# Expert blocks of 64 tokens kept as two halves of 32 and turned on VectorE, with four column groups on TensorE

## The reference, cut to what matters

```python
def expert_block(args):                       # MOE_BLOCK rows of one expert
    xe, e = args
    return (jax.nn.silu(xe @ w_gate[e]) * (xe @ w_up[e])) @ w_down[e]

yb = lax.map(expert_block, (xb.reshape(n_blocks, MOE_BLOCK, dm), blk_expert)).reshape(-1, dm)
y_slot = yb[dest] * wts.reshape(-1)[order][:, None].astype(x.dtype)
return jax.ops.segment_sum(y_slot, tok, num_segments=n_tok)
...
x = x + gate2 * ffn.reshape(bsz, L, D_MODEL)
y_sample = rmsnorm(xs, norm_f_w)
```

## Time and profile before

| | us |
|---|---|
| median of 3 runs | 1439.46 (1433.66 to 1447.06) |
| the profiled execution | 1438.59 |
| its span in the trace | 1436.8 |
| router done, first block's gate products begin | 744.4 |
| last block's down products end | 1406.9 |
| TensorE busy | 1337.9 (93%) |
| VectorE, ScalarE, GpSimd busy | 414.1, 263.3, 235.1 |

### The profile page before, as it was taken

How to read it: one execution, slowest core, us unless ns; L and a number is a source line. 1 busy time by engine, 2 the same in 40 slices (tenths; PEclk the granted TensorE clock), 3 DMA queues, 4 the chain that set the end, 5 groups by cost and what they waited for, 6 DMA issues and landing times.

```text
span 1436.8 us, 25808 instructions
## 1 busy us (share of the span) xinstructions
PE 1337.9 (93%) x10155; PEld 837.8 (58%) x10156; DVE 414.1 (29%) x886; ACT 263.3 (18%) x401; POOL 235.1 (16%) x285
## 2 busy tenths in 40 slices
PE   5899999977999999999958999999999999999975
PEld 3688778756676677764434455555555555454532
DVE  4692870375622210113362000000000000000065
ACT  3305002243125000001111111111111111111102
POOL 0033403200000000000023022012022222223310
PEclk9899999998999999999979999999999999999997
DMA  7459632345430412514088619819949999999993
GB/s 303 150 130 391 149 71 68 80 148 194 148 131 3 177 44 78 215 39 167 15 336 343 257 44 383 340 29 350 393 151 398 379 403 381 404 379 397 383 401 122
DMA packets 92365, 322.30 MB, mean 224 GB/s; under 512 B 12000, under 2 KB 12384, under 8 KB 91536
## 3 DMA queue, kind: packets, MB, share of 16 engines
q1 hardware_dynamic: 72304, 268.77, 49.5%
q0 software_dynamic: 11216, 38.41, 8.7%
q10 hardware_dynamic: 8784, 14.24, 3.2%
HBM read 286.18 MB, written 33.10 MB: 222 GB/s over the span
## 4 chain that ended last, share of the span: by engine, by line
PE 72%; DMA 13%; DVE 5%; issue 3%; SPq 3%; ACT 2%; POOL 0%; POOLq 0%; DVEq 0%; ACTq 0%
PE ps L2236 18%; PE ps L1771 11%; PE ps L2247 10%; PE ps L1759 9%; DMA expert_w<-in_w_down 9%; PE ps L2150 5%; PE ps L2199 5%; SPq L557 3%; PE ps L1863 2%; PE ps L1946 2%; DMA expert_w<-in_w_up 2%; PE ps L2242 1%; DMA x_sorted<-h,router_ints 1%; PE ps L1832 1%; PE ps L2226 1%
## 5 line engine op out<-in xcount | busy, mean ns | idle before, releaser
L2236 PE MATMUL ps<-expert_w,x_block_t 128*64 128x256 f32 x3584 | 403.8, 382 | 15.1 <-issue 6.5
L2236 PEld LDWEIGHTS ps<-expert_w,x_block_t 128*64 128x64 f32 x3584 | 256.0, 137 | 163.1 <-issue 31.5
L2247 PE MATMUL ps<-expert_w,act_t 128*64 128x512 f32 x896 | 213.9, 604 | 3.6 <-DMA expert_w<-in_w_down 2.6
L1771 PE MATMUL ps<-h_t,weight_ring 128*128 128x320 f32 x640 | 178.4, 435 | 0.0
L1771 PEld LDWEIGHTS ps<-h_t,weight_ring 128*128 128x128 f32 x640 | 121.5, 191 | 50.9 <-issue 2.8
L1759 PE MATMUL ps<-h_t,weight_ring 128*128 128x320 f32 x512 | 145.4, 447 | 2.8 <-ACT h_t L749 2.8
L1669 DVE TENSOR_TENSOR activations<-silu_tmp,ps 128x256 f32<-128x256 f32 x56 | 23.6, 421 | 375.9 <-ACT silu_tmp L967 375.9
L1759 PEld LDWEIGHTS ps<-h_t,weight_ring 128*128 128x128 f32 x512 | 100.1, 197 | 45.2 <-issue 6.9
L2247 PEld LDWEIGHTS ps<-expert_w,act_t 128*64 128x64 f32 x896 | 57.8, 136 | 103.1 <-issue 78.2
L692 POOL COPY expert_w<-staged 128x1024 f32<-128x1024 f32 x42 | 43.9, 1044 | 414.5 <-PE ps L2236 269.0
L1690 DVE COPY y_block<-ps 128x512 f32<-128x512 f32 x25 | 17.3, 692 | 188.7 <-PE ps L2247 188.7
(11 more groups left out here) (362 smaller groups left out, 1224.2 us busy)
## 6 DMA issues: line engine op xcount, KB each, us to landing
expert_w<-in_w_down SPq DMA_DIRECT2D x128, 512.0 KB, 13.2
weight_ring<-in_stream SPq DMA_DIRECT2D x98, 512.0 KB, 4.9
expert_w<-in_w_gate SPq DMA_DIRECT2D x58, 512.0 KB, 11.8
expert_w<-in_w_up SPq DMA_DIRECT2D x58, 512.0 KB, 12.8
staged<-in_w_gate SPq DMA_DIRECT2D x28, 512.0 KB, 14.0
gathered<-in_w_gate SPq DMA_DIRECT2D x28, 512.0 KB, 16.0
gathered<-in_w_up SPq DMA_DIRECT2D x28, 512.0 KB, 16.5
x_sorted<-zero POOLq DMA_DIRECT2D x18, 512.0 KB, 13.8
```

What stands on the lines that cost most here:

```text
L1771: last = mm(pair(job)[:, a, :], w[:, k, :], h_t[:, k, a * HALF:(a + 1) * HALF], start=(k == 0), stop=(k == KD - 1))
L2236: last = mm(ps[MB * g:MB * g + MB, 2 * half + w, 0:256], x_blk_t[:, 2 * kp + k2, :], rows[:, at_col:at_col + 256], start=(kp == 0 and k2 = ...
L2247: last = mm(ps[MB * half:MB * half + MB, 4, :], act_t[:, 4 * (f // 4) + 2 * (f % 2) + f // 2 % 2, :], w_slot[3 * f + 2][:, 4 * half:4 * ha ...
```

## The change

A block stays 64 tokens, but as two halves h of 32 (`SUB`). The token operand is 32 columns wide and four column groups (`Q`) run side by side. `gates(h, k)` is four matmuls of 512 columns, which stream 256 columns of the up weight and 256 of the gate weight of input chunk k in one instruction (`w_pair`). Both halves use each chunk in turn, but for the last two, where half 0 uses both and then half 1 both. `down(h, j)` is four matmuls of 256 columns: half 0 with chunks 0 to 3, half 1 with chunks 0 to 3, then both halves in turn with each of chunks 4 to 7. Every output feature of a half now needs all eight input chunks.

The turns of tokens and activations move to VectorE's transpose of 32 x 32 squares: `turn_act(h)` behind each product and `turn_x()` behind both. The rows of the weights are permuted on the host (`expert_rows`) so that these squares put the features where they are needed; ScalarE's three copies per block go. The tokens are loaded, and the results stored, as 128 partitions of 1 KB per half where it was 64 partitions of 2 KB per column half. TensorE's last two blocks are written out like those of the other engines, with `down_both(j)` (two column groups of 64, 512 columns) behind both activations, and the ten selection matrices are turned in the first of the two. For the very first block, VectorE turns the picked tokens straight from PSUM.

```diff
-            def turn_x():
-                for j in range(4):
-                    last = nc.tensor.transpose(ps[:, 6, j * P:(j + 1) * P], x_blk[:, j * P:(j + 1) * P], ident)
-                last.then_inc(xt_done, 1)
-            def turn_act(a):
-                for j in range(2):
-                    last = nc.tensor.transpose(ps[:, 5 + 2 * a, j * P:(j + 1) * P], acts[:, a, j * P:(j + 1) * P], ident)
-                last.then_inc(act_turned, 1)
...
+            def gates(h, k):
+                for g in range(Q):
+                    last = mm(ps[SUB * g:SUB * g + SUB, h, :].rearrange("p (w c) -> p w c", w=2), x_blk_t[:, h, k, :],
+                              w_pair[k][:, :, QC * g:QC * g + QC], start=(k == 0), stop=(k == KD - 1))
+                if h == 1:
+                    last.then_inc(gu_done, 1)
+                elif k == KD - 1:
+                    last.then_inc(half_done, 1)
+
+            both = KD - 2
+            tail_gates = [(0, k) for k in range(both, KD)] + [(1, k) for k in range(both, KD)]
+            tail_downs = [(h, j) for j in range(KF // 2, KF) for h in range(2)]
+
+            def down(h, j):
+                for g in range(Q):
+                    last = mm(ps[SUB * g:SUB * g + SUB, 4 + h, 0:QC], act_t[:, j, h, :],
+                              w_down_sb[j][:, QC * g:QC * g + QC],
+                              start=(j == 0), stop=(j == KF - 1))
+                if h == 1:
+                    last.then_inc(down_done, 1)
+
+            def down_both(j):
                 for half in range(2):
+                    last = mm(ps[MB * half:MB * half + MB, 4, :], act_t[:, j, :, :].rearrange("p h t -> p (h t)"),
+                              w_down_sb[j][:, 512 * half:512 * half + 512],
+                              start=(j == 0), stop=(j == KF - 1))
                 last.then_inc(down_done, 1)
...
             with pe.Fori(1, NBLK) as i:
-                with pe.If(i < blocks):
+                with pe.If(i < last2):
...
+                    for k in range(both):
+                        wait_gates(e, k)
+                        gates(0, k)
+                        gates(1, k)
+                    for h, k in tail_gates:
+                        if h == 0:
+                            wait_gates(e, k)
+                        gates(h, k)
+                    pe.wait_ge(act_ready, i * 2 + 1)
+                    pe.wait_ge(y_copied, i + 1)
+                    for j in range(KF // 2):
+                        pe.wait_ge(dn_in[j], e * 16 + 16)
+                        down(0, j)
+                    pe.wait_ge(act_ready, i * 2 + 2)
+                    for j in range(KF // 2):
+                        down(1, j)
+                    for h, j in tail_downs:
+                        if h == 0:
+                            pe.wait_ge(dn_in[j], e * 16 + 16)
+                        down(h, j)
                 pe.nop()
...
+            for u in range(2):
...
+                pe.wait_ge(y_copied, last2 + (u + 1))
+                if u == 0:
+                    pe.wait_ge(pick_ready, 1)
+                    for n in range(2 * CH):
+                        last = nc.tensor.transpose(ps[:, (7, 5, 6)[n // 4], (n % 4) * P:(n % 4 + 1) * P],
+                                                   pick[:, n // CH, n % CH, :, :].rearrange("p a t -> p (a t)"), ident)
+                    last.then_inc(pick_turned, 1)
+                pe.wait_ge(act_ready, last2 * 2 + (2 * u + 2))
+                for j in range(KF):
+                    pe.wait_ge(dn_in[j], e * 16 + 16)
+                    down_both(j)
...
+            def turn_act(h):
+                vec.transpose(act_t[:, :, h, :], acts[:, h, :].rearrange("p (j l) -> p j l", l=SUB)).then_inc(act_ready, 1)
+
+            def turn_x():
+                vec.transpose(x_blk_t[:, :, :, :].rearrange("p h k t -> p (h k t)"),
+                              x_blk[:, :, :].rearrange("p h c -> p (h c)")).then_inc(xt_copied, 1)
...
             for u, (ahead, beside, behind) in enumerate(((0, 0, 6), (3, 6, 5))):
                 add_some(ahead)
-                dve.wait_ge(silu_ready, last2 * 2 + (2 * u + 1))
-                take_prod(0)
-                add_some(beside)
-                dve.wait_ge(silu_ready, last2 * 2 + (2 * u + 2))
-                take_prod(1)
+                for h in range(2):
+                    dve.wait_ge(silu_ready, last2 * 2 + (2 * u + h + 1))
+                    take_prod(h)
...
             def load_x(row):
-                for g in range(2):
-                    act.dma_start(x_blk[MB * g:MB * g + MB, :], x_sorted[bass.ds(row, MB), 512 * g:512 * g + 512])\
+                for h in range(2):
+                    act.dma_start(x_blk[:, h, :], x_sorted[bass.ds(row + SUB * h, SUB), :].rearrange("t (q c) -> q t c", q=Q))\
                         .then_inc(x_blk_in, 16)
```

More of the change, by code:

```diff
@@ L981, in _ @@
                 with act.If(i < last2):
[L982 to L988, removed]
+                    act.wait_ge(half_done, i + 1)
+                    take_gates(0)
+                    act.wait_ge(gu_done, i * KF + KF)
@@ L1006, in _ @@
[L1006 to L1009 removed]
+                act.wait_ge(half_done, last2 + (u + 1))
+                take_gates(0)
+                act.wait_ge(gu_done, last2 * KF + (u * KF + KF))
+                take_gates(1)
@@ L2223, in _ @@
             pe.wait_ge(pick0_ready, 1)
-            def turn_x():
-                for j in range(4):
-                    last = nc.tensor.transpose(ps[:, 6, j * P:(j + 1) * P], x_blk[:, j * P:(j + 1) * P], ident)
-                last.then_inc(xt_done, 1)
-            def gates(s):
-                half, kp = s // 4, s % 4
-                for k2 in range(2):
-                    for w in range(2):
-                        rows = w_slot[3 * s + w][:, :, :].rearrange("p k c -> p (k c)")
-                        for g in range(2):
-                            at_col = 512 * k2 + 256 * g
-                            last = mm(ps[MB * g:MB * g + MB, 2 * half + w, 0:256], x_blk_t[:, 2 * kp + k2, :],
-                                      rows[:, at_col:at_col + 256], start=(kp == 0 and k2 == 0), stop=(kp == 3 and k2 == 1))
-                last.then_inc(gu_done, 1)
@@ L2309, in _ @@
-                pe.nop()
-            pe.wait_ge(pick_ready, 1)
-            pe.wait_ge(xt_copied, blocks + 1)
-            pe.nop()
-            for n in range(2 * CH):
-                last = nc.tensor.transpose(ps[:, (7, 5, 6)[n // 4], (n % 4) * P:(n % 4 + 1) * P],
-                                           pick[:, n // CH, n % CH, :, :].rearrange("p a t -> p (a t)"), ident)
-            last.then_inc(pick_turned, 1)
+                    for k in range(both):
+                        wait_gates(e, k)
+                        gates(0, k)
+                        gates(1, k)
@@ new lines, in _ @@
+                    for h, j in tail_downs:
+                        if h == 0:
+                            pe.wait_ge(dn_in[j], e * 16 + 16)
+                        down(h, j)
+                pe.nop()
+            for u in range(2):
+                e = pe.value_load(rint[0:1, bass.ds(last2 + u, 1)], min_val=0, max_val=EXPERTS - 1)
+                pe.wait_ge(xt_copied, last2 + (u + 1))
+                for k in range(both):
+                    wait_gates(e, k)
+                    gates(0, k)
+                    gates(1, k)
+                for h, k in tail_gates:
+                    if h == 0:
+                        wait_gates(e, k)
+                    gates(h, k)
+                pe.wait_ge(y_copied, last2 + (u + 1))
+                if u == 0:
+                    pe.wait_ge(pick_ready, 1)
[7 more added lines that the diff above has]
+                    down_both(j)
```

222 lines of the change are left out of this document (96 added, 126 removed).

## The result

The changed kernel takes 1508.46 us (median of 4 runs, 1505.79 to 1516.67) against 1440.76 us for the kernel before on the same chip (median of 4): a ratio of 1.0481, 95% interval 1.0417 to 1.0545. It is slower by 4.8%; the prediction of 1432 us, with a range up to 1451, was wrong. The profiled execution took 1508.03 us with a span of 1506.0 us, 69.2 us more than the 1436.8 of before.

The account below looks back on a forecast made before the run. DMA was taken to bound most of the kernel, TensorE alone only 6.5 of 28 blocks. Terms of -0.3, -9.3, +2.5, +2.6, +1.5 and -4 summed to -7.0 us from 1438.59: 1431.6, said as 1432 for the median, range 1418 to 1451.

Parts of the forecast that it names:

- Tokens and results: Block loads and stores: 256 packets of 2 KB become 512 of 1 KB, 0.44 us more DMA time a block where DMA bounds.
- start: Up to 802.38, DMA bound: last chunk lands where it did, half a down chunk less behind it, -0.3 us.
- three cycles: DMA-bound cycles of two blocks and one: token packets add 1.3 us, a closing DMA gap saves 0.4, +0.9 us each.
- The period: TensorE's time per block: 20.9 us instead of 22.46, with four column groups overlapping; bounds 20.5 and 22.5.
- The turn is covered: Before down: silu, product and VectorE's turn take 1.62 us, just covered by 1.7 of matmuls; rival of no cover, 1442, chance 0.1.
- TensorE-bound stretches and transitions: Middle of the kernel: TensorE-bound stretches save 9.3 us together; three DMA-bound transitions lose 0.85 us each, +2.5.
- The packet's price: Token queue: a line through 4 KB and 2 KB packets gave 63 ns for 1 KB, 0.44 us more a block.
- The skipped iterations: Ahead of the last block but one: nine absent blocks skipped, 5.8 to 10 us of TensorE, 1 us lost.
- The last block: Second product only after six gathered operations, last product at 1412.1, first sum about 1416 against 1420.26: -4 us.
- cycles above 72 (packets): Sign of a wrong forecast: cycles of two blocks and one above 72 us, put down to packets.
- The sign at the end: Sign of a wrong forecast: first sum later after the last weights than the 27.5 us of before.

Follow-up runs that it names:

- e1_spread: Changed kernel with x_block loads and y_sorted stores cut by column group, on 16 DMA engines, same 1 KB packets: 1430.61 us, ratio 0.9931 to the kernel before.
- e5_before_1kb: Kernel before with each block's four transfers cut into eight of 64 x 1 KB, on 16 engines: 1440.4 us, ratio 1.0003.
- e9_before_eight: Kernel before with block loads and stores given an outer dimension of 8, packets still 2 KB: 1466.55 us.
- e7_bound: Changed kernel with transfers on 16 engines, and engine loops ended where the blocks end instead of skipping absent ones: 1429.53 us, ratio 0.9942 to the kernel before.
- e4_before_four: Kernel before with block loads and stores given an outer dimension of 4, packets still 2 KB: 1532.67 us.
- e6_tail: Changed kernel with transfers on 16 engines, and the last block's six gathered operations moved behind its second product: 1428.05 us, ratio 0.9907 to the kernel before.

## Why the prediction was wrong

The step that failed is the term "Tokens and results". It saw that 256 packets of 2 KB become 512 of 1 KB and divided their time by 16 engines ("6.9 us over 16 engines, 0.44 us more DMA time a block"). With 19 DMA-bound blocks that made some 8 us. The diff's `"t (q c) -> q t c"` changed the number of engines too, from 16 to 4, and no rival held that. Measured, this alone is worth 77.0 us, or 3.7 to 4.3 us a DMA-bound block (table below).

The term it should have had, from bytes and a rate of the runs: 4 transfers of 128 KB a block are 524 KB; on 16 engines each carries 33 KB, on four 131. At 386 GB/s over 16 engines (e1_spread's cycle; 391 in the earlier trace rows would do as well), 24.1 GB/s each, the 98 KB more are 4.1 us a block. The chains, stretch by stretch, from one listed block start to the next (second column: the changed kernel less e1_spread; third: the term times the DMA-bound blocks of the stretch; fourth: e1_spread less the kernel before; fifth: what the prediction had for that; all in us). The last row but one runs to the end of the spans, 1436.8 us before, 1506.0 changed and 1429.0 in e1_spread:

| stretch | 4 engines against 16 | by the term | e1_spread against before | predicted |
|---|---|---|---|---|
| start | +0.2 | | +2.0 | -0.3 |
| first transition, with the blocks before it | +9.1 | 2.5 x 4.1 = 10.3 | -2.0 | -2.75 |
| second | +10.7 | 10.3 | -2.5 | -2.75 |
| third | +10.1 | 10.3 | -1.35 | -1.2 |
| three cycles | +11.5, +11.4, +13.0 | 12.3 each | +1.2, +1.2, -0.05 | +0.9 each |
| last two blocks and end | +11.0 | | -6.35 | -2.5 |
| sum | +77.0 | | -7.8 | -6.8 |

The prediction's own sum says -7.0: it entered the three cycles as 2.6, where 3 x 0.9 is 2.7, and rounded twice more. The term needs nothing of the changed kernel but its diff. The 2.0 us at the start stand open, but the start is not firm: in the kernel before it is at 802.38, in e5_before_1kb at 802.37 and in e9_before_eight at 799.09. The starts on which the table rests, of the kernel before as far as the earlier trace rows doesn't have them, and of e1_spread:

```profile
1029.70 8.85 PE ps L2236 x80
...
1120.63 8.85 PE ps L2236 x80
...
1189.11 8.85 PE ps L2236 x80
...
1257.52 8.85 PE ps L2236 x80
```

```profile
804.38 13.94 PE ps L2233 x128
...
916.34 13.94 PE ps L2233 x128
...
1027.20 13.94 PE ps L2233 x128
...
1116.78 13.94 PE ps L2233 x128
...
1186.49 13.94 PE ps L2233 x128
...
1256.12 13.94 PE ps L2233 x128
...
1324.72 13.94 PE ps L2233 x128
```

The Trainium skill, "DMA: Bandwidth & Descriptors", section "Why a DMA increments its semaphore by 16 and not by 1", states the rule: the engines are the largest number up to 16 that divides the slowest dimension (of size above 1) of both access patterns. This case agrees, with 4, 8 and 16 closing packets for outer dimensions of 4, 8 and 32 or 64. The prediction weighed another section of the same page and passed over this one.

The other steps, with the transfers on 16 engines:

- The period: 20.9 forecast, 20.94 and 21.00 measured. Four column groups do overlap on records of 512 columns.
- The turn is covered: in a middle block TensorE is idle for 0.15 us of 21.00 (825.4 to 846.4). The transposes took 446 ns for 256 elements a partition, against the 0.42 assumed (L1659), and 672 ns for 512 (L1662). The prediction's estimate from the Trainium skill, VectorE: DVE Perf Modes, section "The three transpose paths", 0.62 us, was too high for this fp32 shape. Twice the elements took 1.5 times as long, so the time was not in proportion to them.
- TensorE-bound stretches and transitions: right within 0.8 us each in e1_spread. That its whole sum is near the forecast (-7.8 against -6.8) is in part luck: the end gave 3.9 us more than forecast, and the start took 2.3 us more.
- The packet's price: the sign was right and the size wrong, 0.03 us a block instead of 0.44 (e5_before_1kb). The straight line between a 4 KB weight packet and a 2 KB token packet made a fixed cost out of what is a difference between queues; within one queue (q10, 100 ns for 2 KB and 51 ns for 1 KB) the time went with the bytes. The Trainium skill, DMA: Bandwidth & Descriptors, section "Why small descriptors are slow (HBM only)", has the rule that the prediction set aside, by which two packets of 1 KB are an estimated 4% over one of 2 KB. This case agrees: 7.3% against 7.1%. e1_spread's cycles are still 1.2 us longer than before, twice of three, where e5's aren't (68.3, 68.6, 68.2); why was not settled.
- The skipped iterations: 6.41 us of idle time (5.8 to 10 forecast), 6.45 in e1_spread; their effect was put at 1 us, and the time of e7_bound can't tell it from nothing.
- The last block: the second product did wait for the six gathered operations. In e1_spread the first sum came at 1412.51, for the 1416 forecast. In the changed kernel it came only at 1489.43: the late gathers stood ahead of the product.
- In the tests for right and wrong: "cycles above 72 (packets)" named the right sign, and the wrong cause for it; e4_before_four and e5_before_1kb were needed to part them. The sign at the end came true as well: from the last wait for a gate chunk to the first sum the changed kernel took 31.6 us (1457.82 to 1489.43), over the 27.5 of before, and e1_spread 24.5 (1388.0 to 1412.51).

Of the 69.2 us between the profiles, 77.0 are the four engines and -7.8 the rest of the change. The change without that layout, e1_spread, is faster than the kernel before by 0.7% (0.4 to 1.0% by its interval).

## What to carry to other kernels

When a diff rewrites an access pattern of a transfer, count engines before packets: look at its outermost dimension on both sides, and put one there that 16 divides. A small transfer on few engines slows the large ones beside it, as each is landed only with its slowest engine (14 us with only four of 16 at work, mostly on weights, in the changed kernel). The signs are a DMA share that stays at a fraction like 0.26 at the end of a burst, and a queue with fewer closing packets a transfer. And a price per packet is read from one queue, not from a line through two.

## What the hardware showed that was not expected

- A queue that takes 2.7% of the DMA engines' time (q10) held back the weights: its bytes even fell a little (14.24 to 13.72 MB), and the cycles grew by 19%.
- A DMA share of 1.03 doesn't mean the full rate: 372 GB/s in the changed kernel and 399 in the kernel before, at the same share in the same block; with the transfers back on 16 engines it is 390 (e1_spread, 867.4 to 889.0).
- Removing 6.45 us of TensorE's idle time and 5.7 us before the last product gave back less than could be measured. In e7_bound the next limit was a chunk that was issued and landed no earlier than in e1_spread (1369.70 and 1389.58, against 1369.66 and 1388.0 at the latest). In e6_tail it was the 6 us of operations that had been put behind.
